# A one-core hybrid block with a gathered expert mixer: expert slots in pairs through TensorE's column halves, and a new order of slots, dots and front pieces

## The chip, the cores and the metric

The kernel runs on one core of a Trainium2 chip, in one launch. All tensors are float32. The metric is the device time of the whole kernel in microseconds, as the median of several runs. Before the change that is 3865.39 us (3 runs, 3864.82 to 3865.42).

## The reference, cut to what matters

A sequence of 1024 tokens of width 1024 goes through a block with three stages: a token mixer (gated delta net and sliding-window attention side by side), a mixer of single-neuron experts, and a gated embedding. The change is in the expert mixer, and in how the rest is interleaved with it:

```
def block(xb):                                   # 128 tokens
    qr = (xb @ w_query).reshape(128, 8, 2, 128)
    s1, s2 = scores of the two halves of qr against 128 keys each, per head
    v1, i1 = lax.top_k(s1, 16);  v2, i2 = lax.top_k(s2, 16)
    cand = (v1[..., :, None] + v2[..., None, :]).reshape(128, 8, 256)
    sc, ci = lax.top_k(cand, 16)
    eid = e1 * 128 + e2                          # 8 heads x 16 = 128 experts for each token
    gate = jax.nn.softmax(sc, axis=-1)
    hid = jnp.einsum('thkd,td->thk', expert_u[eid], xb)
    act = jax.nn.gelu(hid, approximate=False) * gate
    return jnp.einsum('thk,thkd->td', act, expert_v[eid])
h = h + peer_experts(rms_norm(h, g_ffn), ...)
```

So each token has 128 slots. A slot needs two rows of 4 KB from tables in HBM (`expert_u[eid]` and `expert_v[eid]`), a dot product of length 1024 with the first, and a weighted sum of the second.

## The kernel before, in words

The tokens are cut into 8 tiles of 128. A tile has a **front** (norms, delta net, attention, output projection, query projection, top 16 twice, gates; split into "pieces" per engine) and an **expert phase** (128 slots in 16 groups of G = 8). The expert phase of tile t-1 is interleaved by hand, in program order on each engine, with the front of tile t: the function `tile(t)` of PE (L1184) and of DVE (L1656) alternates one group with one piece. Tiles 2 to 7 of the front are a hardware loop on each engine; tiles 0 and 1 are written out. The last expert phase has no front beside it, but the gated embedding stage.

One group goes like this:

- **POOL** (`gather_group`, L563) copies the group's 8 ids (L567), then issues 8 gathers of `u` rows and 8 of `v` rows (L576). One gather is one slot of all 128 tokens: 128 rows of 4 KB, one per partition. Both rings have 8 buffers. Before every second gather POOL waits until that buffer of the group before is free (`u_used`, `v_used`).
- **DVE** (`experts`, L1642) waits for each `u` row block and makes one dot per slot (L1645), 8 in a row, then waits for the gelu and multiplies by the gate (L1648). Only then does it go on with its front piece.
- **ACT** (`experts`, L813) does the gelu and then builds 8 diagonal matrices of 128x128 (weights of one slot on the diagonal), each after PE has used that buffer's predecessor.
- **PE** (`experts`, L1167) waits for each `v` block and each diagonal, and adds diagonal times rows to the sum in PSUM `expert_sum`: for each slot two matmuls of 512 columns. It does the group before its piece g: PE runs group g-1, then piece g. (In the trace a float32 matmul is two records.)

At the end of a tile DVE copies the new normed rows and gates over (`publish`, L1633), which can be done only when the last dot of the old tile is through, and POOL takes the new ids (`take_ids`, L579). The sum leaves PSUM in `experts_out` (L1650), two copies at L1654.

Pieces of the front that the prediction names: piece0 (PE turns 12 blocks, DVE norms), piece1 and decays_of (gates and decays), piece2 (scaled keys and queries, turned), piece3 and level 1 to 5 (inverse of a triangular matrix: PE, ACT, PE, ACT, PE, DVE for each level), piece6 and piece7 (state), attention_norm, piece8 to piece10 (attention), piece11 and project_out, residual and piece12 (norm), query_pair 0 to 3, best_pair 0 to 3 (top 16), pick (ids), gates.

## Time and profile before

| | |
|---|---|
| median of 3 runs | 3865.39 us |
| the profiled execution's span | 4090.1 us |
| PE busy | 3315.7 us, 81% |
| DVE busy | 2191.8 us, 54% |
| ACT busy | 992.4 us, 24% |
| POOL busy | 2278.2 us, 56% |
| read from HBM, written | 1190.61 MB, 20.77 MB |

The profiled execution is longer than the timed runs (4090.1 against 3865.39 us), so a time worked out in it has to be scaled. PE is TensorE (its weight loads stand apart as PEld), DVE VectorE, ACT ScalarE, POOL GpSimd, SP SyncE. A name as L894 is a line of the kernel; L894 is the helper through which nearly all matmuls go and L897 the one for transposes, so PE's groups are told apart by the tiles they write and read. "Idle before" is time in which the engine stood still ahead of instructions of that group, with what released it.

### The profile page before, as it was taken

Reading aid. Unit: us, or ns where it says so; the run is one execution under the profiler, and the core shown is the slowest. Engines: PE = TensorE matmul, PEld = TensorE weight load, DVE = VectorE, ACT = ScalarE, POOL = GpSimd, SP = SyncE. Lnnn points to the kernel's source line nnn. Section 1 sums busy time; section 2 is a strip of 40 time slices with the busy share of each in tenths; the row PEclk is TensorE's granted clock in tenths of the full one; section 3 lists DMA queues with packets and bytes.
Section 4 is the critical chain, followed back from the end, with each engine's and each line's share of the span. In section 5 each row is a group of like instructions: output and inputs, shape, how many; then the busy total and the mean of one; then the engine's idle time right before and its main releaser. Section 6 shows DMA issues by size and latency. Waiting matters only on the chain.

```text
span 4090.1 us, 38210 instructions
## 1 busy us (share of the span) xinstructions
PE 3315.7 (81%) x11032; PEld 1816.9 (44%) x11032; DVE 2191.8 (54%) x4881; ACT 992.4 (24%) x2278; POOL 2278.2 (56%) x2189
## 2 busy tenths in 40 slices
PE   8997757897788787887879778877888687969999
PEld 4444535453444344443535344444545253534444
DVE  1124285567444854477456744486357644574543
ACT  2112213222222132212221222212221222213332
POOL 0000055667556775767566755676566656666764
PEclk9998778898889897898889888898899798989999
DMA  3321187899789998899889978899799979999996
GB/s 125 118 75 63 39 298 263 309 363 389 264 302 335 362 358 289 316 346 365 280 313 373 365 269 297 318 360 342 278 324 369 356 260 322 352 364 373 381 355 243
DMA packets 413927, 1214.00 MB, mean 297 GB/s; under 512 B 43680, under 2 KB 137888, under 8 KB 413600
## 3 DMA queue, kind: packets, MB, share of 16 engines
q0 software_dynamic: 294912, 1073.87, 71.6%
q1 hardware_dynamic: 118816, 137.66, 9.9%
q8 instruction: 103, 1.69, 0.2%
q14 instruction: 96, 0.79, 0.1%
HBM read 1190.61 MB, written 20.77 MB: 296 GB/s over the span
## 4 chain that ended last, share of the span: by engine, by line
PE 54%; DVE 14%; issue 13%; DMA 7%; POOL 5%; ACT 4%; another core or an unknown queue 2%; SPq 1%; POOLq 0%; DVEq 0%; ACTq 0%
PE expert_sum L894 28%; PE bank L894 23%; DVE u_rows L1645 5%; DMA u_rows<-in_peer_u_dram,group_ids 4%; DMA w_query<-in_peer_w_query_dram 3%; PE bank L897 3%; POOL u_rows L576 3%; POOL v_rows L576 2%; ACT weight_diagonals L610 1%; ACT L610 1%; ACT arena L610 1%; DVE arena L1420 1%; DVE arena L1552 1%; DVE arena L1537 1%
## 5 line engine op out<-in xcount | busy, mean ns | idle before, releaser
L894 PE MATMUL expert_sum<-v_rows,weight_diagonals 128*128 128x512 f32 x4096 | 1871.7, 617 | 153.0 <-ACT weight_diagonals L610 116.9
L576 POOL DMA_INDIRECT v_rows<-in_peer_v_dram,group_ids x1024 | 1191.1, 1163 | 827.7 <-PE expert_sum L894 541.8
L1645 DVE CUSTOM_DVE_ANT_0 u_rows<-u_rows,ffn_in 128x1024 f32<-128x1024 f32 x1024 | 1215.7, 1225 | 454.8 <-DMA u_rows<-in_peer_u_dram,group_ids 410.3
L894 PEld LDWEIGHTS expert_sum<-v_rows,weight_diagonals 128*128 128x128 f32 x4096 | 810.4, 200 | 1161.7 <-issue 1078.0
L576 POOL DMA_INDIRECT u_rows<-in_peer_u_dram,group_ids x1024 | 1052.3, 1028 | 416.8 <-issue 371.0
L897 PE MATMUL bank<-constants,arena 128*128 128x128 f32 x968 | 184.5, 336 | 330.2 <-DVE arena L1475 82.4
L610 ACT ACTIVATE weight_diagonals<-constants,expert_weight 128x128 f32<-128x128 f32 x1024 | 331.7, 390 | 228.5 <-PE expert_sum L894 177.4
L894 PE MATMUL bank<-w_query,arena 128*128 128x256 f32 (+1 forms) x1088 | 297.6, 436 | 87.4 <-DMA w_query<-in_peer_w_query_dram 50.6
L610 ACT ACTIVATE gelu<-hidden 128x8 f32<-128x8 f32 x128 | 26.7, 208 | 1386.1 <-DVE hidden L1645 1237.0
L897 PEld LDWEIGHTS bank<-constants,arena 128*128 128x128 f32 x968 | 139.1, 171 | 392.6 <-issue 212.2
L894 PEld LDWEIGHTS bank<-w_query,arena 128*128 128x128 f32 x1088 | 231.6, 215 | 155.7 <-issue 59.6
L589 POOL CAST expert_id<-expert_id_new 128x32 uint32<-128x32 f32 x1 | 0.2, 209 | 522.1 <-DVE expert_id_new L1602 522.1
L894 PE MATMUL bank<-arena 128*128 128x128 f32 (+4 forms) x2176 | 252.2, 295 | 40.1 <-issue 23.0
L894 PEld LDWEIGHTS bank<-arena 128*128 128x128 f32 (+3 forms) x2176 | 240.7, 201 | 60.5 <-issue 47.0
L894 PE MATMUL bank<-w_out_sb,arena 128*128 128x512 f32 x512 | 235.2, 615 | 21.9 <-ACT arena L861 10.4
L610 ACT ACT_TABLE_LOAD x172 | 220.7, 1283 | 3.8 <-PEq L1751 0.7
L1420 DVE COPY_PREDICATED arena<-constants,bank 128x512 f32<-128x512 uint32 x80 | 58.1, 726 | 287.3 <-PE bank L894 131.6
L894 PE MATMUL bank<-normed_by_channel,w_channel 128*128 128x512 f32 x384 | 167.2, 598 | 0.5 <-issue 0.5
L894 PEld LDWEIGHTS bank<-w_out_sb,arena 128*128 128x128 f32 x512 | 99.5, 197 | 146.7 <-issue 132.7
L894 PE MATMUL bank<-w_token,normed_tile 128*128 128x512 f32 (+1 forms) x384 | 142.4, 532 | 0.0
L1513 DVE TENSOR_TENSOR arena<-arena,bank 128x512 f32<-128x512 f32 x16 | 11.0, 688 | 203.5 <-PE bank L894 173.0
L894 PEld LDWEIGHTS bank<-normed_by_channel,w_channel 128*128 128x128 f32 x384 | 73.7, 193 | 93.6 <-issue 93.6
(166 smaller groups left out, 1968.1 us busy)
## 6 DMA issues: line engine op xcount, KB each, us to landing
w_query<-in_peer_w_query_dram SPq DMA_DIRECT2D x64, 1024.0 KB
u_rows<-in_peer_u_dram,group_ids POOLq DMA_INDIRECT x1024
v_rows<-in_peer_v_dram,group_ids POOLq DMA_INDIRECT x1024
w_channel<-in_w_in_dram SPq DMA_DIRECT2D x12, 512.0 KB
conv_scratch<-conv_out SPq DMA_DIRECT2D x12, 512.0 KB, 2.6
arena<-conv_scratch SPq DMA_DIRECT2D x8, 768.0 KB
tok_scratch<-token_out SPq DMA_DIRECT2D x8, 648.0 KB
arena<-tok_scratch SPq DMA_DIRECT2D x8, 648.0 KB
```

Source lines behind the costliest of these rows:

```text
L576: nc.gpsimd.indirect_dma_start(ring[:, j, :], None, table, bass.IndirectOffsetOnAxis(ids[:, half, j:j + 1], 0)).then_inc(landed[j], 16)
L589: nc.gpsimd.tensor_copy(eid[:, 0:EARLY * G], eid_new[:, 0:EARLY * G]).then_inc(first_ids_taken, 1)
L610: return nc.scalar.activation(out_, in_, func, **kw)
L894: return nc.tensor.matmul(out_, lhsT, rhs, start=start, stop=stop, **kw)
L897: return nc.tensor.transpose(out_, in_, ident)
L1420: v.copy_predicated(invT[:, 4 * r:4 * r + 4, :], level_mask(l), bank[3 + r][:, :].rearrange("p (s n) -> p s n", n=P)).then_inc(invT_ready, 1)
L1513: v.tensor_tensor(h1[:, n * 512:n * 512 + 512], x_t[:, n * 512:n * 512 + 512], bank[n][:, :], ALU.add).then_inc(h1_ready, 1)
L1537: last = v.max_index(index[:, first], top[:, first], row)
L1552: last = v.max_index(index[:, second], top[:, second], row)
L1645: v.tensor_tensor_reduce(u_ring[:, j, :], u_ring[:, j, :], xb[:], 1.0, 0.0, ALU.mult, ALU.add, hid[:, g * G + j:g * G + j + 1]).then_inc(u ...
```

## The change

1. **Paired slots.** The slots of one token are taken in pairs. PE turns ids, gates and normed rows over with identity halves (`ids_to_pairs`, `gates_to_pairs`, `rows_to_pairs`), so that partition 64 s + i of buffer j = 2m + b holds token 64 b + i and its slot 2m + s. A gather still fetches 128 rows. The weight matrix of a buffer is then 128x64 (two slots of 64 tokens), and its products go to the 64 partitions b of the sum. Four matmuls of 512 columns serve a pair of buffers, as before, but with 64 weight columns each, b = 0 and b = 1 in turn.
2. **Weights by DVE.** ACT no longer builds diagonals. DVE makes the weights of half a group with one multiplication of a constant 0/1 matrix (`C_REP`) with the weights, into two sets of buffers.
3. **Sums one group behind.** In step q, DVE begins with two dots of group q, then the weights of group q-1 (`begin`). PE does the slots of group q-1 in one block, then its piece. ACT's gelu of group q-1 comes in step q too.
4. **Dots spread.** The other six dots of a group are laid one or two at a time ahead of DVE's waits inside the front piece (`fill`); what is left follows the piece.
5. **Front re-cut** into pieces by new borders: piece9 with piece10, piece11 with project_out(1), level 5 with piece6 and piece7, and so on. The last step of a tile has no piece on any engine.
6. **POOL** issues in pairs, `v` of group q-1 and `u` of group q in turn, straight from `eid`, which has two sets now. The copies of ids and the `publish` copies are gone; ACT copies ids, gates and rows out of PSUM.
7. **No loops** over tiles are left in this part; everything is written out.
8. For the very first tile PE turns ids over only after all of its query pairs.

The core of the diff, PE and DVE:

```diff
-                for j in range(G):
-                    pe.wait_ge(v_landed[j], (t * NG + g + 1) * 16)
-                    pe.wait_ge(diag_ready, t * SLOTS + g * G + j + 1)
-                    for n in range(2):
-                        last = mm(acc[:, n * 512:n * 512 + 512], diag[:, j, :], v_ring[:, j, n * 512:n * 512 + 512],
-                                  False, g == NG - 1 and j == G - 1)
...
+                for pair in range(PAIRS):
+                    for b in range(NB):
+                        pe.wait_ge(v_landed[pair * NB + b], (q + 1) * 16)
+                    pe.wait_ge(diag_ready, 2 * q + (pair * NB) // GP + 1)
                     for n in range(2):
...
+                        for b in range(NB):
+                            last = mm(acc[b * B:b * B + B, n * 512:n * 512 + 512], diag[:, q % 2, pair * NB + b, :],
+                                      v_ring[:, pair * NB + b, n * 512:n * 512 + 512], False,
+                                      g == NG - 1 and pair == PAIRS - 1)
...
+            def expert_weights(q, half):
...
+                dve.wait_ge(gelu, 2 * q + half + 1)
+                v.tensor_tensor(act_w[:, q % 2, cols], gel[:, q % 2, cols], gate[:, e % 2, g * G + cols.start:g * G + cols.stop],
+                                ALU.mult).then_inc(weights_ready, 1)
+                dve.wait_ge(weights_ready, 2 * q + half + 1)
...
+                v.tensor_tensor(diag[:, q % 2, cols, :], cst[:, C_REP:C_REP + B].unsqueeze(1).broadcast_to([P, GP, B]),
+                                act_w[:, q % 2, cols].unsqueeze(2).broadcast_to([P, GP, B]), ALU.mult).then_inc(diag_ready, 1)
...
+            def begin(q):
+
+                fill(2)
+                if q:
+                    expert_weights(q - 1, 0)
+                    expert_weights(q - 1, 1)
...
             def level(t, l):
                 for r in range(2):
+                    fill(2 if r == 0 else 1)
                     dve.wait_ge(level_p, 10 * t + 2 * (l - 1) + r + 1)
...
+            for q in range((NT - 1) * NG):
+                dots = expert_dots(q)
+                begin(q)
...
+                for i in front_piece(q):
+                    pieces[i](q // NG + 1)
+                fill(G)
```

and POOL:

```diff
+            for q in range(NP):
+                e, g = divmod(q, NG)
+                late = e > 0 and g == 0
...
+                for pair in range(PAIRS):
+                    if q and not late:
+                        gather_v(q - 1, pair)
+                    gather_u(q, pair)
```

PE's main loop: for each q, the block of slots of group q-1 (`finish_slots`), then the piece. In steps 14 and 15 of a tile PE turns ids, gates and rows over. `fill` stands in PE's pieces too, but the block ahead of the piece has taken all slots by then.

## Rows read from the trace of the kernel before

**Rows 1.** Groups by line and shape: busy us, mean ns, idle before.

```profile
L894 PE MATMUL expert_sum<-v_rows,weight_diagonals 128*128 128x512 f32 x4096 | 1871.7, 617 | 153.0 <-ACT weight_diagonals L610 116.9 <-issue 36.0
...
L1564 DVE TENSOR_TENSOR arena<-arena 128x256 f32<-128x256 f32 x64 | 24.4, 424 | 14.2 <-remote 10.0 <-DVE arena L1552 3.4
...
L1648 DVE TENSOR_TENSOR expert_weight<-gelu,gate 128x8 f32<-128x8 f32 x128 | 21.9, 171 | 35.2 <-ACT gelu L610 32.2 <-issue 3.0
```

**Rows 2.** Timeline of DVE: the sum leaves PSUM, tiles 0 and 5.

```profile
1001.53 1.29 DVE L1654 COPY ffn_in_new<-expert_sum 128x512 f32<-128x512 f32 x2
...
3228.07 1.29 DVE L1654 COPY ffn_in_new<-expert_sum 128x512 f32<-128x512 f32 x2
```

**Rows 3.** Windows: us; busy PE, PEld, DVE, ACT, POOL; clock, DMA share, GB/s.

```profile
1450.00:1895.00 445.00, 357.48 (x1230) 201.03 (x1231) 260.96 (x594) 110.55 (x271) 292.20 (x277) 0.88 0.91 330
...
3671.00:4060.00 389.00, 360.44 (x871) 162.30 (x871) 189.60 (x320) 113.92 (x229) 257.33 (x258) 0.96 0.96 365
```

**Rows 4.** Timeline of PE in a steady tile: blocks of slots.

```profile
1511.32 13.90 PE L894 MATMUL expert_sum<-v_rows,weight_diagonals 128*128 128x512 f32 x32
...
1539.76 15.54 PE L894 MATMUL expert_sum<-v_rows,weight_diagonals 128*128 128x512 f32 x32
```

**Rows 5.** Who waited for whom: total us, times, longest us.

```profile
POOL v_rows L576 <- PE expert_sum L894: 541.8, 195, 22.7
...
DVE u_rows L1645 <- DMA u_rows<-in_peer_u_dram,group_ids: 410.3, 216, 13.3
```

**Rows 6.** Timeline of PE: a front product in column halves begins, twice.

```profile
468.35 0.45 PE L894 MATMUL bank<-arena,values_before 128*64 128x128 f32 x4 [0.68 <-ACT arena L768]
...
1675.53 0.70 PE L894 MATMUL bank<-arena,values_before 128*64 128x128 f32 x4 [0.68 <-ACT arena L768]
```

**Rows 7.** Windows over those two products, columns as in rows 3.

```profile
468.30:470.30 2.00, 1.95 (x32) 1.78 (x32) 0.00 (x0) 0.00 (x0) 0.00 (x0) 1.00 0.04 8
...
1675.50:1679.00 3.50, 3.47 (x32) 3.34 (x32) 0.00 (x0) 0.00 (x0) 2.21 (x4) 0.50 0.89 308
```

**Rows 8.** Timeline of DVE: dots; a best_pair; pick and gates.

```profile
573.04 1.23 DVE L1645 CUSTOM_DVE_ANT_0 u_rows<-u_rows,ffn_in 128x1024 f32<-128x1024 f32 x1
...
574.19 1.22 DVE L1645 CUSTOM_DVE_ANT_0 u_rows<-u_rows,ffn_in 128x1024 f32<-128x1024 f32 x1
...
505.40 0.87 DVE L1532 MAX8 arena<-arena 128x8 f32<-128x128 f32 x4 [15.36 <-ACT arena L797]
...
516.89 0.20 DVE L1576 CAST arena<-arena 128x64 f32<-128x64 uint32 x1
...
1410.47 0.23 DVE L1576 CAST arena<-arena 128x128 f32<-128x128 uint32 x1
...
1420.89 1.22 DVE L1645 CUSTOM_DVE_ANT_0 u_rows<-u_rows,ffn_in 128x1024 f32<-128x1024 f32 x1
```

**Rows 9.** Timelines of PE and DVE: front of tile 0, without experts.

```profile
367.02 2.80 PE L897 MATMUL bank<-constants,arena 128*128 128x128 f32 x12 [16.11 <-DMA arena<-conv_scratch]
...
401.14 0.73 DVE L1420 COPY_PREDICATED arena<-constants,bank 128x512 f32<-128x512 uint32 x1 [5.16 <-PE bank L894]
...
406.40 0.73 DVE L1420 COPY_PREDICATED arena<-constants,bank 128x512 f32<-128x512 uint32 x1 [3.59 <-PE bank L894]
...
503.52 1.33 PE L894 MATMUL bank<-keys_by_channel,arena 128*128 128x128 f32 x8
```

**Rows 10.** Timeline of PE: two levels with experts beside, written out.

```profile
681.68 3.78 PE L894 MATMUL bank<-arena 128*128 128x128 f32 x32
...
693.75 13.90 PE L894 MATMUL expert_sum<-v_rows,weight_diagonals 128*128 128x512 f32 x32
```

**Rows 11.** Timelines of POOL and PE: first gather; end of tile 0's queries.

```profile
523.98 1.09 POOL L576 DMA_INDIRECT u_rows<-in_peer_u_dram,group_ids  x1 [0.94 <-POOL group_ids L567]
...
535.78 0.94 PE L894 MATMUL bank<-keys_by_channel,arena 128*128 128x128 f32 x4 [0.71 <-issue]
```

**Rows 12.** Windows: the 25 us with the densest DMA, columns as in rows 3.

```profile
1800.00:1825.00 25.00, 17.05 (x54) 11.10 (x52) 20.62 (x59) 3.96 (x14) 17.67 (x17) 0.86 1.03 401
```

More of the change, by code:

```diff
@@ L607, in _ @@
+            for pair in range(PAIRS):
+                gather_v(NP - 1, pair)
         @block.scalar
@@ L827, in _, with experts @@
+            def experts(q):
+                for half in range(2):
+                    cols = slice(half * GP, half * GP + GP)
+                    act.wait_ge(u_used, q * G + cols.stop)
+                    f(gel[:, q % 2, cols], hid[:, q % 2, cols], ACT.Gelu).then_inc(gelu, 1)
+            first, rest, whole = slice(0, EARLY * G), slice(EARLY * G, SLOTS), slice(0, SLOTS)
+            for piece in pieces[:9]:
                 piece(0)
             normed_T(0)
-            for pair in range(3):
+            for pair in range(4):
@@ L830, in _ @@
                 query_pair(0, pair)
-            piece_gate(0, slice(0, EARLY * G))
-            query_pair(0, 3)
-            for g in range(FIRST):
-                experts(0, g)
-            piece_gate(0, slice(EARLY * G, SLOTS))
-            for i, group in enumerate(merged(pieces)):
-                experts(0, FIRST + i)
-                for piece in group:
-                    piece(1)
-            with act.Fori(2, NT) as t:
-                for g in range(NG):
-                    experts(t - 1, g)
-                    pieces[g](t)
+            take_rows(0)
@@ L1191, in _, with fill, finish_slots @@
+            slots = iter(())
+            credit = 0
+            def fill(n):
+                nonlocal credit
+                credit += n
+                while credit >= 2:
+                    credit -= 2
+                    next(slots, None)
+            def finish_slots():
+                for _ in slots:
+                    pass
             pe.wait_ge(rel_rows_ready, NH)
+            first, rest, whole = slice(0, EARLY * G), slice(EARLY * G, SLOTS), slice(0, SLOTS)
             for piece in pieces:
@@ L1193, in _ @@
                 piece(0)
-            for g in range(FIRST - 1):
-                experts(0, g)
-            for i, group in enumerate(merged(pieces)):
-                experts(0, FIRST - 1 + i)
-                for piece in group:
-                    piece(1)
-            experts(0, NG - 1)
-            with pe.Fori(2, NT) as t:
-                tile(t)
+            rows_to_pairs(0)
+            ids_to_pairs(1, first)
+            pe.wait_ge(first_gates, 1)
+            gates_to_pairs(first)
@@ new lines, in _ @@
+            for q in range((NT - 1) * NG):
+                t = q // NG + 1
+                slots = expert_slots(q - 1) if q else iter(())
+                credit = 0
+                if q % NG == NG - 1:
+                    rows_to_pairs(t)
+                finish_slots()
+                for i in front_piece(q):
+                    pieces[i](t)
+                if q == 1:
+                    ids_to_pairs(3, rest)
+                    pe.wait_ge(vector_front, 1)
+                    gates_to_pairs(rest)
+                if q % NG == NG - 2:
+                    ids_to_pairs(2 * t + 3, whole)
+                    pe.wait_ge(vector_front, t + 1)
+                    gates_to_pairs(whole)
@@ L1650, in experts_out, with fill @@
+            dots = iter(())
+            def fill(n):
+                for _ in range(n):
+                    next(dots, None)
+            def begin(q):
+                fill(2)
+                if q:
+                    expert_weights(q - 1, 0)
+                    expert_weights(q - 1, 1)
+                if q > NG and q % NG == 1:
+                    experts_out(q // NG - 1)
             def experts_out(t):
[L1652 removed]
+                dve.wait_ge(v_used, (t + 1) * SLOTS // NB)
+                if t < NT - 1:
+                    dve.wait_ge(rows_mm, 2 * NB * (t + 2))
```

388 lines of the change are left out of this document (225 added, 163 removed).

## The prediction

> **What bounds the kernel now.** I read the page's costly groups first, then the stretches by tile, the order of blocks and pieces on PE, and the waits. PE is busy for 1871.7 us of the 4090.1 with the products of the experts' sum, 128 groups of 14.6 us [rows 1]. A steady tile takes 445.3 us: the sum leaves PSUM at 1001.53 and, five tiles on, at 3228.07 [rows 2]. In such a tile PE is busy 357 of 445 us and the DMA engines 0.91 at 330 GB/s; in the last one, without a front, PE has 360 of 389 us and DMA 0.96 at 365 GB/s [rows 3]. PE runs a block of slots (13.9 to 15.5 us), then its piece: from the block's end at 1525.2 the next begins at 1539.76, 14.5 us for two levels [rows 4]. The largest waits behind PE are POOL's for free `v` buffers (541.8 us); DVE's for `u` rows are 410.3 us [rows 5]. So PE's chain of block and piece sets the steady time, with DMA close behind, and DVE sets the stretch with the top 16.
>
> **Part 1, the block of slots.** The number of matmuls stays at 2048, but two with 64 columns of weights can run side by side. A front product has this form already, 128 rows by 64 weight columns, 128 moving columns, halves in turn: beginning at 468.35 and at 1675.53 [rows 6]. Its 32 records keep PE busy for 1.95 us at a granted clock of 1.00 and for 3.47 us at 0.50 [rows 7], so at full clock a record comes every 0.061 us, while a record of a full array costs 13.90 / 32 = 0.434 us for 512 columns [rows 4], 0.109 for 128. That is a factor of nearly 2. No row shows it with 512 moving columns. Bounds for a block: 14.6 us (no gain) and 7.0 (half of 13.9); I take 7.3, half the mean, since the row nearest in form has the full factor. The work is off PE for 117 us a tile.
>
> **Part 2, what is late next.** Before, the weights of group g-1 were there when PE came, and DVE's end of a piece ran beside PE's block. Now PE's block in step q waits for `begin(q)` on DVE, which comes after DVE's whole piece of step q-1: two dots at 1.15 (573.04 to 574.19), a product of 0.17, a weight build of 256 columns, for which I take the 0.42 of a sum of that size, and an estimated 0.3 for the waits between: 3.2 us [rows 1, 8]. Then the block, then PE's piece, then DVE's end of it, in series. So a step costs the piece's bare chain plus 3.2 plus 7.3. The bare chain is to be seen in tile 0, whose front ran with no experts: from the first turn at 367.02 to the scores of query pair 0 at 504.85 it took 137.8 us [rows 9]. That is steps 0 to 9:
> - bare chain 137.8; less 5 for products of piece2 and for attention_norm, which DVE can do beside PE's block;
> - ten blocks: 73;
> - ten times 3.2 ahead of the block, less 3.7 in step 8, where PE is still turning probabilities: 28;
> - dots laid in waits that don't hide them. DVE idles 3.59 us ahead of a level, which holds two dots of 1.15; the third one, between the two halves of a level, costs 1.1, five times; some ten others stand in gaps about as short as themselves, an estimated 1 each: together 15 [rows 8, 9];
> - h1 added to the sum, four records of 0.43: 2;
> - delays that the bare chain doesn't have: two levels took 12.1 us from 681.68 to 693.75 with experts beside them, in written-out code [rows 10], against 10.5 alone (401.14, two levels at 5.26) [rows 9]. I take 15% of 137.8: 20.
>
> Sum 271 us. Bounds of the last term: 0, and 38% (14.5 against 10.5) as in the loop [rows 4], 52.
>
> **Part 3, steps 10 to 14 belong to DVE.** 40 dots 46; five times the weights of both halves 7.5; four best_pair at 11.5 (505.40 to 516.89) 46; two picks and the gates, 10.4 (1410.47 to 1420.89) and 9: 19.4; split dots 2; less 4, as step 10 begins beside PE's step 9: 117 [rows 1, 8]. Nothing is gained there, and ACT's builds of diagonals go from an engine with room. **Step 15** has no piece: DVE and PE are soon done and the round of 16 gathers decides. A gather is 0.524 MB; at 365 / 0.96 = 380 GB/s [rows 3] it takes 1.38 us, 22 for the round. Some short steps (2, 9) reach this floor too: 4.
>
> A steady tile then takes 271 + 117 + 22 + 4 = 414 us, 31.3 less, six times: -188. POOL's copies of ids and the drain at the end of a tile are in this difference. The unrolled code and two more sets of buffers cost nothing that a row shows; two levels took less in written-out code than in the loop, 12.1 against 14.5 [rows 4, 10].
>
> **Part 4, the ends.** The first gather now goes out at 523.98, while PE's queries of tile 0 last until 536.7 [rows 11]. After the change ids are turned over only after these, the turned rows (8 matmuls, 3.5 us in halves) and some copies by ACT: near 545, 21 to 22 us later, and DVE stands still for it: +22. Expert phase 0, mostly without the loop already: 0, bounds -30 and +30. The last tile now takes 24.3 us a step with PE at 93% [rows 3]; with a block of 7.3 the DMA round of 22 us is the next limit: 16 x 22.1 + 2 = 356 against 389: -33. The sum one group behind at the very end: +3.
>
> Sum: 4090.1 - 188 + 22 + 0 - 33 + 3 = 3894 us profiled. The median is 0.9451 of the profiled span (3865.39 / 4090.1); scaled, 3680 us.
>
> **Rivals.**
> - *DMA is the bound.* If DVE's ends of pieces hide better than in my sum, transfers limit: a tile moves 445 x 330 = 146.9 MB [rows 3], at 380 GB/s 386 us; the densest 25 us moved 401 GB/s [rows 12], which gives 366. With 386: 4090.1 - 356 + 22 - 30 - 33 + 3 = 3696, scaled 3493 (with 366: 3380). For it: DMA already has a share of 0.91. Against: the series in part 2.
> - *The new wait takes back all of it.* If the pieces stretch by 38% as in the loop, the tile is 446 us: 4090.1 + 4 + 22 + 20 - 33 + 3 = 4106, scaled 3881. For it: dots wait for `u` rows ahead of the front's work on DVE, so that a late gather now holds the front as well (410.3 us of such waits) [rows 5].
> - *Slower: PE's clock.* PE will stand still more, ahead of each block above all. In the stretch at 1675.5, after PE had waited for probabilities, the granted clock was 0.50 [rows 7], its lower level of 1.2 GHz, and records took twice as long. A block at half clock lasts 14 us. With two thirds of the ten blocks' time so, 44 us are added: tile 458, 4090.1 + 76 + 22 + 30 - 33 + 3 = 4188, scaled 3958. It decides from a mean block of 10.4 us on (31.3 / 10 more than 7.3). Against: blocks now lose 0.7 us on average (14.6 against 13.9) though PE waits ahead of them too [rows 1, 4].
> - *The halves don't run side by side at 512 columns.* Ten blocks cost 73 us more: tile 487, last tile as before: 4090.1 + 250 + 22 + 50 + 3 = 4415, scaled 4173.
>
> The Trainium skill, TensorE: Matmul & The Clock Gate, Part 1, says that the array's clock is gated by activity and that gaps between bursts bring it back to the half rate; by that rule, which the row at 1675.5 bears out, the clock rival holds and 3958 us is its time. The Trainium skill, DMA: Bandwidth & Descriptors, Specifications, gives a limit of about 358 GB/s from HBM per core, by which a tile could not go below 410 us and the DMA rival would be out; the last tile's mean of 365 GB/s disagrees [rows 3], and the measurement decides.
>
> **How the numbers follow.** The forecast (tile of 400 to 432 us) gets 0.53; the DMA bound 0.15; the new wait 0.17; the clock 0.10; no concurrency 0.05. The range, 3470 to 3890 us, reaches from just under the DMA case to just over the new wait's; it leaves out the two slow cases and the far end of the fast one, some 0.2. The bounds of the 15% term alone are 3567 and 3862 (six tiles of -20 and +32 us, scaled). A measurement of this kernel tells 0.2% from no change. Faster: forecast and DMA case, and 0.07 of the new wait: 0.75. Within 0.2%: 0.05. Slower: 0.20.
>
> **What would show it.** In the profile of the changed kernel: blocks of 32 records in 7 to 8 us (over 10: clock; 14: no concurrency); PE's products of the sum near 940 us; between piece and block on PE a wait of 3 us for DVE's weights; steps 5, 7 and 8 the longest, over 28 us; the sum leaving PSUM every 414 us; DMA near 355 GB/s in a steady tile; the first gather near 545. A tile under 395 us with a DMA share near 1 would make part 2 wrong; a DVE that waits for `u` rows inside its pieces would make the second rival right.

## The result, and the profile after

The changed kernel took 4007.3 us (median; 3987.2 to 4008.0) beside 3865.4 for the kernel before: a ratio of 1.035, 95% interval 1.033 to 1.037. It is slower by 142 us. The forecast was 3680 us, so the change came out 327 us above it.

From its page and its groups (answering to [rows 1]): the span; the busy share of each engine; the shares of the chain of work that ended last; then the group of the sum with out<-in, shape and count, busy us and mean ns of one, idle time before them and what ended it.

```profile
span 4005.3 us, 34568 instructions
...
PE 2609.5 (65%) x11304; PEld 1355.7 (34%) x11304; DVE 2239.5 (56%) x5248; ACT 688.0 (17%) x1425; POOL 2323.0 (58%) x2052
...
PE 42%; DVE 22%; DMA 18%; issue 11%; POOL 4%; ACT 3%; SPq 1%; DVEq 0%; POOLq 0%; ACTq 0%
...
L920 PE MATMUL expert_sum<-v_rows,weight_diagonals 128*64 128x512 f32 x4096 | 1135.0, 710 | 837.2 <-DVE weight_diagonals L1765 678.0
```

The halves do run side by side: PE's busy time in the sum fell from 1871.7 us to 1135.0, a mean block from 14.6 to 8.87 us (1135.0 / 128). But PE now waits 678 us for DVE's weights, and its busy share of the span fell from 81% to 65%. Who waited for whom, in all (total us, times, longest), beside [rows 5]:

```profile
PE expert_sum L920 <- DVE weight_diagonals L1765: 678.0, 121, 29.7
...
POOL v_rows L591 <- PE expert_sum L920: 386.6, 86, 30.7
...
DVE u_rows L1780 <- DMA u_rows<-in_peer_u_dram,expert_id: 310.0, 124, 13.1
...
PE expert_sum L920 <- DVE ffn_in_new L1807: 93.1, 7, 13.9
```

Windows over a steady tile and the last one, columns as in [rows 3], and DVE's timeline where the sum leaves PSUM after the first tile, the seventh and the last:

```profile
1465.90:1892.40 426.50, 263.23 (x1253) 138.30 (x1253) 264.64 (x637) 68.58 (x153) 293.51 (x256) 0.79 0.93 341
3607.00:3977.00 370.00, 287.52 (x868) 113.24 (x868) 187.76 (x346) 71.96 (x110) 256.92 (x240) 0.88 0.96 364
```

```profile
1039.74 1.28 DVE L1807 COPY ffn_in_new<-expert_sum 128x512 f32<-128x512 f32 x2
...
3607.21 1.28 DVE L1807 COPY ffn_in_new<-expert_sum 128x512 f32<-128x512 f32 x2
...
3977.44 1.29 DVE L1807 COPY ffn_in_new<-expert_sum 128x512 f32<-128x512 f32 x2 [11.77 <-PE expert_sum L920]
```

Six steady tiles are 3607.21 - 1039.74 = 2567.5 us, 427.9 each, and the last one is 370.2.

One thing must be known to read these numbers: the same program takes different times on different chips. The execution of the kernel before that stands ahead of the prediction lasts 4090.1 us, its timed runs 3865.4; those of the change agree with its profile (4005.3 and 4007). The experiments met two kinds of chip: on A (the result's), D and F the kernel before takes 3865 to 3874 us, on B, C and E 4084 to 4132. The profile of before that the prediction read is like those of the second kind. What differs is shown under experiments 2 and 3; numbers are compared here on one chip, or on chips where the kernel before takes the same. Each letter stands for one chip at one time: no run tells whether the chip itself makes the difference or something that happened there then, such as other work beside it.

### The profile page after: what moved, and what is told of

Read it like the earlier page. It is cut to its first block, busy times and chain, and to the rows that moved or that the text cites. A ratio compares the mean times of both kernels' runs of the same rounds, so it can differ in the third digit from the quotient of the medians.

```text
span 4005.3 us, 34568 instructions
## 1 busy us (share of the span) xinstructions
PE 2609.5 (65%) x11304; PEld 1355.7 (34%) x11304; DVE 2239.5 (56%) x5248; ACT 688.0 (17%) x1425; POOL 2323.0 (58%) x2052
## 4 chain that ended last, share of the span: by engine, by line
PE 42%; DVE 22%; DMA 18%; issue 11%; POOL 4%; ACT 3%; SPq 1%; DVEq 0%; POOLq 0%; ACTq 0%
PE bank L920 23%; PE expert_sum L920 16%; DMA w_query<-in_peer_w_query_dram 11%; DVE u_rows L1780 7%; DMA v_rows<-in_peer_v_dram,expert_id 3%; DMA u_rows<-in_peer_u_dram,expert_id 3%; POOL u_rows L582 2%; PE bank L923 2%; POOL v_rows L591 2%; DVE arena L1530 1%; ACT L616 1%; DVE arena L1713 1%; DVE arena L1719 1%; DVE arena L1722 1%; ACT arena L616 1%
## 5 line engine op out<-in xcount | busy, mean ns | idle before, releaser
L582 POOL DMA_INDIRECT u_rows<-in_peer_u_dram,expert_id x1024 | 1196.3, 1168 | 967.4 <-ACT expert_id L821 539.4
L920 PE MATMUL expert_sum<-v_rows,weight_diagonals 128*64 128x512 f32 x4096 | 1135.0, 710 | 837.2 <-DVE weight_diagonals L1765 678.0
L591 POOL DMA_INDIRECT v_rows<-in_peer_v_dram,expert_id x1024 | 1126.5, 1100 | 675.8 <-PE expert_sum L920 386.6
L1780 DVE CUSTOM_DVE_ANT_0 u_rows<-u_rows,ffn_in 128x1024 f32<-128x1024 f32 x1024 | 1222.5, 1218 | 313.1 <-DMA u_rows<-in_peer_u_dram,expert_id 310.0
L920 PEld LDWEIGHTS expert_sum<-v_rows,weight_diagonals 128*64 128x64 f32 x4096 | 367.7, 161 | 1551.8 <-issue 1551.4
L923 PE MATMUL bank<-constants,arena 128*128 128x128 f32 x968 | 171.3, 318 | 251.7 <-DVE arena L1625 85.9
L920 PE MATMUL bank<-arena 128*128 128x128 f32 (+4 forms) x2176 | 234.9, 282 | 18.6 <-DVE arena L1530 13.4
L920 PEld LDWEIGHTS bank<-arena 128*128 128x128 f32 (+3 forms) x2176 | 222.7, 189 | 42.6 <-issue 26.2
L1759 DVE TENSOR_TENSOR expert_weight<-gelu,gate 128x4 f32<-128x4 f32 x256 | 40.6, 159 | 280.7 <-ACT gelu L616 280.6
L795 ACT COPY arena<-bank 128x256 f32<-128x256 f32 x64 | 23.8, 372 | 583.6 <-PE bank L920 583.6
L1765 DVE TENSOR_TENSOR weight_diagonals<-constants,expert_weight 128x256 f32<-128x256 f32 x256 | 108.9, 426 | 8.8
```

The lines of the kernel that those rows point to most:

```text
L582: nc.gpsimd.indirect_dma_start(u_ring[:, j, :], None, table_u, bass.IndirectOffsetOnAxis(id_of(q, j), 0)).then_inc(u_landed[j], 16)
L591: nc.gpsimd.indirect_dma_start(v_ring[:, j, :], None, table_v, bass.IndirectOffsetOnAxis(id_of(q, j), 0)).then_inc(v_landed[j], 16)
L920: return nc.tensor.matmul(out_, lhsT, rhs, start=start, stop=stop, **kw)
L923: return nc.tensor.transpose(out_, in_, ident)
L1759: v.tensor_tensor(act_w[:, q % 2, cols], gel[:, q % 2, cols], gate[:, e % 2, g * G + cols.start:g * G + cols.stop], ALU.mult).then_inc(wei ...
L1765: v.tensor_tensor(diag[:, q % 2, cols, :], cst[:, C_REP:C_REP + B].unsqueeze(1).broadcast_to([P, GP, B]), act_w[:, q % 2, cols].unsqueeze( ...
```

## The experiments

All runs under one heading were made on one chip, with the kernel before beside them.

### 1. Chip B (before: 4131 us): loops, and three ways to undo the wait

The kernel before with its loops over tiles written out:

```diff
-            with pe.Fori(2, NT) as t:
+            for t in range(2, NT):
```

> The kernel before with the loops over tiles 2 to 7 (and POOL's over groups) written out on all five engines, nothing else changed. The profiled execution of before lasts 4090.1 us, its timed runs 3865.4; the change, whose tiles are written out, lasts 4005.3 profiled and 4007 timed. Theory L (loops cost time only while they are profiled): the timed run stays near 3865 (within 10 us), the profiled span falls to within 10 us of it, a steady tile then shows about 408 us (445.3 less 225 / 6) and two levels take about 12 us where the loop's took 14.5. Rival M (loops help the unprofiled run, for instance by shorter code to fetch): the timed run rises to about 4000. Rival N (the difference comes from POOL's copies of ids or ACT's diagonals, which the change drops, not from loops): the profiled span stays near 4090 with a timed run near 3865.

Measured: 4093.7 us, ratio 0.991 (0.988 to 0.994), profiled span 4080.1. None of the three theories holds. The profiled span and the time of this kernel agree, and the kernel before takes 4131 here. Loops cost some 37 us on this chip; they are not where the 225 us between profile and time lie.

Dots and weights of a group in its own step, as before the change:

```diff
 def begin(q):
-    fill(2)
-    if q:
-        expert_weights(q - 1, 0)
-        expert_weights(q - 1, 1)
+    fill(G)
+    expert_weights(q, 0)
+    expert_weights(q, 1)
```

> The change, but DVE does all 8 dots of group q, then its weights and diagonals, at the head of step q, ahead of its piece (as before the change), and ACT its GELU there; PE still sums group q-1 in step q, in column halves. PE then finds the weights ready. Theory W (the series DVE piece, two dots, weights, PE block, PE piece is what the change lost; it waits 678 us for weights): these waits fall under 150 us, the steady tile of 426 us goes to about 400, the time to about 3830. Rival S (the dots spread over the piece's waits are worth as much as the wait costs): the steady tile stays within 8 us of 426, the time between 3950 and 4060. Rival D (DMA, at a share of 0.93, is the bound): tile no lower than 415, time no lower than 3920.

Measured: 4333.9 us, ratio 1.049 (1.038 to 1.060). PE's wait for weights fell to 7 us in all, and the time is that of the change (4338 on chip C, where before takes the same 4132). That is what rival S foretold, that eight dots ahead of DVE's piece put into the series what the wait took out. But this run changes a second thing. DVE copies the sum out only behind its eight dots and weights, and PE waits for that copy before it can begin the next tile's sum; first this run, then the change on C:

```profile
PE expert_sum L918 <- DVE ffn_in_new L1804: 255.9, 7, 40.5
...
PE expert_sum L920 <- DVE ffn_in_new L1807: 94.0, 7, 14.4
```

So 162 us of new waits stand at the seven tile borders, and how much of the rest the dots took is not separated.

PE sums two groups behind (POOL fetches the `v` rows one step later too, and DVE copies the sum out one step later):

```diff
-                slots = expert_slots(q - 1) if q else iter(())
+                slots = expert_slots(q - 2) if q > 1 else iter(())
```

> The change, but PE sums the slots of group q-2 in step q (and POOL gathers their v rows there), so that the weights made in step q-1 are there when PE comes; dots stay spread. Theory W: the 678 us of waits for weights mostly go, about half of them, 340 us, leave the path: steady tile about 395, time about 3800. Rival D (DMA bound): tile 410 to 420, time 3890 to 3960, DMA share 0.96 or more. Rival C (what follows is DVE's and PE's chain of the piece anyway, so only PE's place of waiting moves, to its first turn or product of each piece): time 3980 to 4010, waits for arena tiles on PE grow by what those for weights lose.

Measured: 4121.4 us, ratio 0.997 (0.994 to 1.001). Against the change's 1.051 on chip C that is 5% won back without moving a dot. The times of 3800 (theory W) and 3980 to 4010 (rival C) were meant for a chip of the first kind; experiment 5 has that run.

PE's slots in the waits of its piece:

```diff
-                finish_slots()
                 for i in front_piece(q):
                     pieces[i](t)
+                finish_slots()
```

> The change, but PE's slots of a group are laid in the waits of its piece (a pair of slots at every second place marked there, what is left at the piece's end) and not as one block ahead of it. Theory W: PE's piece still stands behind weights, but only a pair of slots of 2.2 us lies between it and DVE's next operation, so the block leaves the chain in steps with several turns: steady tile 426 less about 20, time about 3870. Rival B (a block is the better place: v buffers come free later, and pairs of slots hold up turns for which DVE waits): time 4030 or more, POOL's waits for v buffers above 387 us.

Measured: 4006.9 us, ratio 0.969 (0.961 to 0.976), 8% under the change's ratio on C. Theory W in kind: of the single choices undone on this chip, the block ahead of the piece cost the most.

### 2. Chip C (before: 4132): the two kernels again, and the change taken apart

> The kernel before, unchanged, for its own trace beside a time of the same chip. On one chip its timed runs took 3865 us (within 1 us of each other), on the chip of the written-out version, another one, 4107 to 4179, and the profiled span of 4090 us is like the latter. Theory K (the kernel before has two speeds, by chip, and the trace that the forecast was read from is of the slower one): the profiled span equals the time of its own chip within 30 us, whichever that is; where it is near 3865, the trace shows which stretch is shorter. Rival P (a profile costs 225 us on the fast chip): span near 4090 beside times near 3865.

> The change, unchanged, on the same chip as the kernel before. It took 4007 us where before took 3865. Theory K: before is the one that varies, the change stays within 30 us of 4007, so that on a chip where before takes 4130 the change is faster by 3%, and on one where before takes 3865 slower by 3.5%. Rival: the change varies as before does, the ratio stays 1.035, and the time on the slower chip is near 4275.

Measured: before 4130.9 us, profiled span 4117.8; the change 4337.8, ratio 1.051 (1.045 to 1.056). Theory K held for the profile and fell for the change: it varies as before does, and more (8% against 7%). Its two executions, on A and C, are the same program. Up to the first gather they agree within 0.4 us (539.9 and 540.2); after it a tile takes 428 us on A and 471 on C. The engines' own durations are alike: a dot has a mean of 1218 and 1219 ns, a record of the sum 710 and 714. The timeline of all engines shows what differs. First chip A: PE's products of a level, ACT's two copies, then DVE's masked copy, which waits for PE's second product:

```profile
1550.68 3.88 PE L920 MATMUL bank<-arena 128*128 128x128 f32 x32
...
1551.87 0.58 ACT L731 COPY arena<-bank 128x512 f32<-128x512 f32 x1 [11.32 <-PE bank L920]
...
1552.77 0.59 ACT L731 COPY arena<-bank 128x512 f32<-128x512 f32 x1 [0.31 <-PE bank L920]
...
1553.82 0.73 DVE L1530 COPY_PREDICATED arena<-constants,bank 128x512 f32<-128x512 uint32 x1 [9.18 <-PE bank L920]
```

And the same place on chip C, with a window over it:

```profile
1613.63 3.15 PE L920 MATMUL bank<-arena 128*128 128x128 f32 x24
...
1614.98 0.59 ACT L731 COPY arena<-bank 128x512 f32<-128x512 f32 x1 [12.51 <-PE bank L920]
...
1619.29 0.59 ACT L731 COPY arena<-bank 128x512 f32<-128x512 f32 x1 [3.72 <-remote]
1619.93 0.97 PEld L920 LDWEIGHTS bank<-arena 128*128 128x128 f32 x8 [3.34 <-issue]
...
1625.12 0.72 DVE L1530 COPY_PREDICATED arena<-constants,bank 128x512 f32<-128x512 uint32 x1 [17.24 <-remote]
```

```profile
1615.50:1625.50 10.00, 2.44 (x18) 1.94 (x16) 0.38 (x1) 0.66 (x2) 5.49 (x6) 0.81 1.02 401
```

PE had ended the 24 products at 1616.8 us; ACT's copy, due 0.3 us after its half, started 3.7 us late, and DVE's, due at 1617, at 1625.1, though both engines stood idle. The semaphore's own record has its change at 1625.0: the signal landed late. "Remote" and "issue" in such rows name no engine; they mean that no end of work stands beside the change.

How often this happens can be counted. For each of the 5268 signals that PE, DVE and ACT raise after the first gather I took the next recorded change of its semaphore: in the trace of C it comes over 0.5 us after the instruction's end for 1167 of them, on A for 3. (An upper bound, as records are missing: C's trace lists 31,042 changes of semaphores, A's 42,917 for the same program.) The trace of before that the prediction read is of the late kind too, with 1637 of 6229 by the same count. So are all twelve traces taken on B, C and E, with 16 to 34%; the six of A, D and F have three such signals at most.

The change without column halves:

```diff
-B = 64
+B = 128
```

> The change without its column halves: one slot at a time with 128 columns of weights, as in the kernel before; everything else of the change stays (dots spread, sums one group behind, slots as one block ahead of the piece, weights on DVE). A block lasts 13.9 to 15 us. Theory B (in the series of steps 0 to 9 the block's length counts in full): 128 blocks x 5.5 us less what hides in steps 10 to 15, some 10 of 16 steps in 7 tiles, the last tile too: 4007 + 7 x 55 + 60 = 4450 us. Rival H (half of a block hides beside DVE's work): 4200. Against the kernel before this shows what spreading and the later sum cost or bring by themselves: faster than before only if under its time.

Measured: 4794.7 us, 457 over the change on this chip. A mean block has 2041.6 / 128 = 15.95 us instead of 8.9:

```profile
L920 PE MATMUL expert_sum<-v_rows,weight_diagonals 128*128 128x512 f32 x4096 | 2041.6, 662 | 707.8 <-DVE weight_diagonals L1765 482.3 <-issue 206.7 <-DMA v_rows<-in_peer_v_dram,expert_id 18.8
```

Theory B: ten blocks in each of seven tiles are 70 x 7.0 = 491 us. In the order of the change the block stands in the series nearly in full. And without the halves that order is 663 us slower than before on this chip; the halves only pay for part of it.

Weights ahead of the dots:

```diff
 def begin(q):
-    fill(2)
     if q:
```

> The change, but the weights of group q-1 come first in DVE's step q, not behind two dots of group q. Theory W (two dots of 1.2 us are in the series ahead of the block): in ten steps of a tile 2.4 us less, of which about 1.2 come back as waits for ACT's GELU: 12 us a tile, 80 to 90 in all, time 3920. Rival R (DVE then waits for the GELU as long as the dots last, or the dots taken out have to be done later in the same series): no change within 15 us of the change's own time.

Measured: 4338.0 us, the change's own time. Rival R: the two dots cost nothing where they are. Without them DVE waits longer for ACT's GELU, 444 us in all by the rows of waits (246 ended by ACT, 197 by nothing named) against 301 in the change on C.

### 3. Chip D (before: 3870): the kernel before, traced on a chip without late signals

> The kernel before, unchanged, again for the trace of a further chip. So far two chips gave 4131 us and one 3865. In the traces of the slow ones a part of the engines' signals land late: a semaphore that PE raised at 1616.8 us reached DVE at 1625.0, where the trace of the change at 4007 us shows delays of 0.01 us throughout. Theory K2 (late signals make the slow chips slow, for every kernel): where the time is near 3865, the trace shows no share of issue and unknown queue above that of the change's fast trace (11%), two levels in the loop take about 10.5 to 12 us instead of 14.5, and a steady tile takes about 408 to 415 us; where it is near 4130, the trace is as the two before it (445 to 450 a tile).

Measured: 3874.2 us, span 3861.4. Theory K2. Of 6228 signals one is late by the count above. Windows over a steady tile and the last, and PE's timeline over two levels:

```profile
1397.40:1811.20 413.80, 346.61 (x1225) 193.32 (x1224) 260.38 (x591) 105.99 (x260) 289.26 (x275) 0.90 0.95 350
3462.70:3832.00 369.30, 355.88 (x869) 160.62 (x870) 183.32 (x308) 113.40 (x228) 248.10 (x250) 0.98 0.97 370
```

```profile
1459.71 13.90 PE L894 MATMUL expert_sum<-v_rows,weight_diagonals 128*128 128x512 f32 x32
1473.45 3.78 PE L894 MATMUL bank<-arena 128*128 128x128 f32 x32
...
1483.91 13.90 PE L894 MATMUL expert_sum<-v_rows,weight_diagonals 128*128 128x512 f32 x32
```

A tile has 413 us (986.4 to 3462.7 in six), not 445. Two levels in the loop take 24.20 - 13.90 = 10.3 us, not the 14.5 of [rows 4], and in the written-out tile 1 they take 10.5 (671.86 to 682.32), not the 12.1 of [rows 10]; tile 0 alone has 10.5. What the prediction took for the loop's price and for the company of experts were late signals.

> The change with PE's slots laid in the waits of the piece, as in the earlier run (4007 us where the kernel before took 4131, ratio 0.969). Theory W (the block ahead of the piece is what the change lost, on any chip): ratio 0.95 to 0.98 on a slow chip again; on a fast one, where the change takes 4007 and before 3865, 3800 to 3860. Rival B (the gain comes only from cover against late signals): on a fast chip not faster than the change's 4007.

> The change with both: PE sums group q-2 in step q, and its slots lie in the waits of the piece (h1 is added at the head of the step). Theory W: neither weights nor the block stand in the series any more, only pairs of slots of 2.2 us that hold up a turn by one on average: 20 to 60 us under the version with slots in the pieces alone, near 3960 on a slow chip, 3760 on a fast one. Rival D (that version is bound by DMA already, whose share of its steady tile is to be 0.93 or more): no change against it within 15 us.

Measured: 3874.8 us, ratio 1.000 (0.998 to 1.002), and 3840.9 us, ratio 0.991 (0.988 to 0.994). On this kind of chip slots in the pieces bring 132 us against the change's 4007 on A and merely reach the kernel before, above theory W's 3800 to 3860; rival B is out. With the sums two groups behind as well the kernel before is beaten, by 0.9%: 34 us under the slots alone, as theory W had it, though far from its 3760. Windows of that last version, a steady tile and the last one (15 steps, as the sum leaves a step later):

```profile
1442.70:1846.10 403.40, 276.19 (x1253) 138.07 (x1253) 266.95 (x636) 68.73 (x153) 291.92 (x254) 0.81 0.96 359
3473.00:3814.00 341.00, 270.26 (x843) 102.41 (x843) 176.00 (x325) 66.58 (x103) 253.03 (x227) 0.90 0.98 376
```

### 4. Chip E (before: 4084): what a halved block is worth by itself

In the kernel before, each slot goes into half of the sum's columns, so that the block is halved and the other half of the columns lacks its experts:

```diff
-                    for n in range(2):
+                    for n in range(2 if g == NG - 1 and j == G - 1 else 1):
                         last = mm(acc[:, n * 512:n * 512 + 512], diag[:, j, :], v_ring[...],
```

> The kernel before (loops, order, full-array slots unchanged) with half of its slots' work left out: each slot is multiplied into columns 0 to 511 of the sum alone (the last slot of a tile into both halves), so that a block lasts 7 us instead of 13.9, as column halves at full clock would make it; the other half of the sum's columns lacks its experts. It measures what a halved block is worth with nothing else of the change. Theory B (the block is in PE's series in ten steps of a tile): 48 to 69 us less a tile, near 3480 where the kernel before takes 3870, near 3740 where it takes 4131. Theory D (on the fast chip a tile of 412 us has the DMA engines at 0.95 already, and 16 rounds of gathers at 23 us leave 370 to 400): tile about 400, time 3760 to 3800 there, and a larger gain, 100 to 250 us, on a slow chip, where DMA has more room.

> The change with PE's sums two groups behind and its slots in the waits of the piece, again: 3841 us on a fast chip (0.991 of before). Theory T (this order has slack for signals that land late, as the version with slots in the pieces alone, which lost 132 us on the slow chip where before lost 261): on a slow chip 3950 to 4000 and a ratio of 0.955 to 0.97; on a fast one 3830 to 3850 again. Rival: it loses as much as before, 4100.

> The change with PE's sums two groups behind, the slots still as one block: 4121 us on a slow chip, where the change takes 4337. Theory W (waits for weights cost the change 5% on any chip): on a fast chip 3850 to 3900 against the change's 4007. Rival L (two thirds of those 216 us are late signals that fall on the added wait): 3930 to 3970 on a fast chip. On a slow one 4110 to 4130 again.

> The change, unchanged, beside the three others of this call on one chip: 4007 us where the kernel before takes 3870, 4337 where it takes 4131.

Measured: half block 4027.3 us, ratio 0.987 (0.981 to 0.994); both measures 3913.5, 0.959 (0.953 to 0.965); two behind alone 4099.6, 1.004 (1.001 to 1.008); the change 4350.3, 1.062 (1.054 to 1.070). The half block gave 57 us, less than either theory: with late signals two levels took 30.1 and 25.8 us. The order that wins on D wins by more here: it is 73 us slower than on D, where the kernel before is 214 slower and the change, against A, 343. Its trace has no fewer late signals than that of the change (32% against 20%). That they cost most where waits stand in one series fits these numbers; no run singles it out.

### 5. Chip F (before: 3867): the same two without late signals

> As the run before it with half of the slots' work left out (each slot into columns 0 to 511 alone), which gave 4027 us where the kernel before took 4084: there pieces grew by as much as blocks shrank, two levels took 26 to 30 us with signals that landed late. On a chip without late signals: theory D (DMA at 0.95 to 0.97 of the kernel before bounds it) gives 3790 to 3830 where before takes 3870; theory B (PE's series) under 3600. On a chip with late signals near 4030 again.

> As the run of the change with PE's sums two groups behind and one block, which gave 4100 where the change took 4350. On a chip without late signals theory W gives 3850 to 3900 (the change 4007), rival L 3930 to 3970; on a chip with them 4100 again.

Measured: half block 3735.1 us, ratio 0.965 (0.963 to 0.967); two behind 3884.8, 1.005 (1.003 to 1.008), in theory W's range and 122 us under the change on A. Most of the 678 us of waits did not become time: PE still stands 596 us ahead of the sum's products (837 in the change), 526 of them ended by nothing that the profile names. By the code PE waits there for `v` rows and for weights, and the weights were made a step earlier. Here 24 records run and the 8 of the last pair of `v` buffers come after 3.6 us:

```profile
1522.29 5.37 PE L921 MATMUL expert_sum<-v_rows,weight_diagonals 128*64 128x512 f32 x24
...
1531.29 3.10 PE L921 MATMUL expert_sum<-v_rows,weight_diagonals 128*64 128x512 f32 x8 [3.63 <-issue]
```

So 122 us is what a later sum with later `v` gathers brings; the price of the wait for weights by itself was not measured.

PE's timeline over two levels of the half-block kernel, ACT's in the same step, and windows over a steady tile, that step and the last tile:

```profile
1433.02 7.03 PE L894 MATMUL expert_sum<-v_rows,weight_diagonals 128*128 128x512 f32 x16
1439.88 1.95 PE L894 MATMUL bank<-arena 128*128 128x128 f32 x16
1446.12 3.78 PE L894 MATMUL bank<-arena 128*128 128x128 f32 x16 [4.28 <-ACT arena L725]
...
1456.74 7.03 PE L894 MATMUL expert_sum<-v_rows,weight_diagonals 128*128 128x512 f32 x16
```

```profile
1442.63 0.21 ACT L610 ACTIVATE gelu<-hidden 128x8 f32<-128x8 f32 x1 [8.83 <-DVE hidden L1645]
1443.15 2.44 ACT L610 ACTIVATE weight_diagonals<-constants,expert_weight 128x128 f32<-128x128 f32 x8 [0.31 <-DVE expert_weight L1648]
1445.50 1.04 ACT L725 COPY arena<-bank 128x512 f32<-128x512 f32 x2
```

```profile
1391.00:1788.00 397.00, 254.55 (x967) 153.54 (x967) 261.10 (x590) 104.21 (x260) 290.54 (x274) 0.79 0.98 367
...
1433.00:1456.70 23.70, 19.06 (x98) 14.10 (x97) 12.88 (x22) 7.11 (x17) 17.46 (x20) 0.86 1.03 408
3364.70:3718.60 353.90, 271.21 (x615) 123.33 (x616) 182.85 (x308) 113.47 (x228) 246.84 (x251) 0.85 1.00 388
```

The block is 6.9 us shorter and the step 0.5 us: 23.72 against 24.20. Two things took the rest. In the order before, DVE does its eight dots while PE does its block, and ACT then does the GELU and builds eight diagonals (2.44 us) ahead of its copy for the level; with half the block gone PE stands 4.3 us for that copy. And of the level's products the 16 behind this wait take 3.78 us where the 16 ahead of it took 1.95: the granted clock is 0.86 in the step, 1.00 in the same step on D. The change has no diagonals on ACT, so this run prices a halved block in the kernel before and not in the change.

A steady tile has 398 us in the mean of six (394 to 405), 14 us less than on D, with the DMA engines at 0.98. Theory D was right about the tile (about 400) and 55 us too high in its time (3790 at the least); B is out. That transfers bound this tile is read from their share; no run varied them.

## Why the prediction was wrong

**The scale to the runs.** This is the step that failed, and it made two thirds of the miss: 3894 - 3680 = 214 us. The factor 0.9451 was 3865.39 / 4090.1, and it was laid on a sum whose largest terms had nothing to be scaled: the start of tile 0 (first gather at 524.0 in the trace that was read, 523.0 on D), blocks (13.90 in both) and dots are the same on both kinds of chip. The gap was in the late signals of the trace, and those lie in the tile of 445 us that the forecast tile replaced. On a chip without them the kernel before has 413 us, and the forecast of 414 was no gain at all. So it does not hold that a time worked out in that trace has to be scaled. Left unscaled, the prediction's own sum says 3894 beside 3865: slower. The warning was in the table of times: timed runs within 1 us of each other and a profiled execution 225 us away can't be one condition.

**The sum by terms**, forecast against the change's trace, with the kernel before on D. The forecast column lays the prediction's differences (-188, +22, -33, +3) on the rows of the trace that it read, where the sum leaves at 1001.5, 3682.9 and 4059.4:

| stretch, us | forecast | change (A) | before (D) |
|---|---|---|---|
| until the first tile's sum leaves | 1023.5 | 1039.7 | 986.4 |
| six steady tiles | 2493.4 | 2567.5 | 2476.3 |
| last tile | 343.5 | 370.2 | 369.3 |
| after it | 33.7 | 27.9 | 29.4 |
| span | 3894.1 | 4005.3 | 3861.4 |

The third of the miss that is left, 4005 against 3894 unscaled, is in the first three lines and is taken part by part.

**Part 1** held in kind. No row had shown halves with 512 columns side by side; they run so, and at full clock a block takes 7.09 us (the one at 1765.80), as taken. The mean is 8.87, since a block begins after a wait. The records of the sum (ns min/median/max), and a window over a step of two levels:

```profile
L920 PE MATMUL expert_sum<-v_rows,weight_diagonals x4096: 592/593/1117, 573.6 to 3976.3; 128*64 128x512 f32 x196
```

```profile
1541.90:1565.30 23.40, 18.88 (x112) 12.25 (x113) 12.80 (x25) 4.88 (x10) 18.52 (x17) 0.93 0.98 361
```

Half the records take 593 ns or less, the longest 1117, and the mean is 710 (607 in the kernel before on D). In a step of two levels the granted clock is 0.93, with DVE's wait in it, where it was 1.00 in the same step before. The rule of the Trainium skill, TensorE: Matmul & The Clock Gate, Part 1, holds in direction: gaps between bursts cost clock. The clock rival, which it carried, decided from 10.4 us on; at 8.87 it took 10 x 1.57 = 16 us a tile, and is a part of the loss, not its cause. The front's products paid nothing: those with `w_query` have a mean of 427 ns in both.

**Part 2, steps 0 to 9**, was nearly right as an absolute sum: 271 us forecast, 263.5 measured (blocks at 1442.67 and 1706.20). Its terms in a step of two levels, PE's timeline of the change:

```profile
1541.96 8.78 PE L920 MATMUL expert_sum<-v_rows,weight_diagonals 128*64 128x512 f32 x32 [2.23 <-DVE weight_diagonals L1765]
1550.68 3.88 PE L920 MATMUL bank<-arena 128*128 128x128 f32 x32
1554.60 0.66 PE L923 MATMUL bank<-constants,arena 128*128 128x128 f32 x4
1556.35 0.66 PE L923 MATMUL bank<-constants,arena 128*128 128x128 f32 x4 [1.10 <-DVE arena L1530]
...
1565.30 8.78 PE L920 MATMUL expert_sum<-v_rows,weight_diagonals 128*64 128x512 f32 x32 [2.23 <-DVE weight_diagonals L1765]
```

The step has 23.34 us where before has 24.20: the block is 5.1 us less; from the last product to the block there are 2.88 us, 2.4 more than before, for the weights; and 0.86 more in each of the two levels, where a dot lies between the halves of DVE's masked copy (1554.60 to 1556.35, 1.75 us; before 0.89). The excess of 15% isn't there: two levels take 10.3 us plus those 4.1. It made up for the longer blocks. What the prediction missed is what the step was to be compared with: before, the block lay beside DVE's dots, and the step was PE's and DVE's at once. The half-block run shows it for the kernel before, where half a block gives this step 0.5 us.

The term for h1 was mis-sized: it had four records, 2 us, where PE waits in each tile as well, 93.1 us in seven:

```profile
1893.74 3.78 PE L920 MATMUL expert_sum<-arena,constants 128*128 128x512 f32 x4 [13.88 <-DVE ffn_in_new L1807]
```

The sum can't restart before DVE has copied it out, and DVE comes to that only after the last six dots of step 0, two of step 1 and the weights (1881.6 to 1892.4). This wait is part of the 263.5.

**Part 3** missed by 13 us in steps 10 to 14 (129.9 against 117) and by 7 in step 15 (32.9, from 1836.1 to the block at 1869.0, against 22 and 4). Windows over both:

```profile
1706.20:1836.10 129.90, 77.28 (x324) 40.30 (x325) 107.80 (x329) 11.23 (x33) 90.30 (x78) 0.82 0.99 368
1836.10:1870.00 33.90, 11.57 (x36) 3.45 (x38) 11.87 (x22) 2.34 (x6) 22.37 (x23) 0.70 1.03 403
```

DVE is busy for 107.8 of 129.9 us, and the DMA engines are full. With one set of buffers they cannot fetch ahead in steps 0 to 9 (their share is 0.90 from 1466 to 1706) and, so it seems, become the limit in the rest; no run with more buffers tells.

In the last tile the prediction read its baseline wrongly: its window of 389 us begins 12 us before the sum leaves, and by the sum the tile is 376.5. So its 16 rounds of 22.1 and 2 (356) became 343.5 in the sum. Measured are 370.2, that is 23.1 us a round at 364 GB/s, as before on D. The round of 22.1 itself is reached: the half-block kernel's last tile takes 353.9 us at a share of 1.00 and 388 GB/s. So the 380 GB/s, from busy share and rate, holds for a tile without a front. Beside a front no steady tile shown here moves more than 367.

**Part 4.** The start: first gather at 539.9, forecast near 545, 17 us later than the 523.0 of D. Expert phase 0 was put at nothing and costs 1039.7 - 986.4 - 17 = 36 us; no run tells which of its steps lose it.

**The rivals.** "The new wait takes back all of it" is what happened, and its price, 3881 us after scaling, was 126 short. PE waits 678 us for weights, and the runs two groups behind give 122 us back on a chip without late signals and 216 to 251 with them. That it put the tile at 446 was the late signals again; it is 428. DMA as the bound fits what could be won, with another number: steady tiles have 398 us in the half-block kernel at a share of 0.98 and 406 in the best whole one, where 386 was priced. That halves don't run side by side fell. On every chip where it ran, the change is slower (1.035, 1.051, 1.062).

The Trainium skill, DMA: Bandwidth & Descriptors, Specifications, has about 358 GB/s per core; here the mean is 367 over a steady tile of 397 us and 388 over a last tile of 353.9, so the measurement differs and decides. As a bound for a tile (410 us by it) it was passed too, with the 398 and 406 above; the 386 was not reached.

## What to carry to other kernels

Before a profiled execution is scaled to the timed runs, ask what the gap is made of; a sum built from bare durations has no such gap, and must be compared with a baseline taken in the same condition. Halving an engine's block is worth what the block has in the series: where other engines work beside it, first read what they do in the same time (here half a block gave a step 0.5 of 6.9 us). And an order that puts weights, block and piece in one series can cost more than the halved block brings: on chip C the order cost 663 us and the halves won back 457. With the sum one group later still and the block cut into the waits of the piece, 3.5% slower (A) became 0.9% faster (D), and 6.2% slower became 4.1% faster (E).

## What the runs showed of the hardware that was not expected

- One program's time differs from chip to chip: the kernel before takes 3865 to 3874 and 4084 to 4132 us (5.4 to 6.9%), the change 4007 and 4338 to 4350 (8.2 to 8.6%), the order with both measures 3841 and 3913 (1.9%). The engines' own durations are alike. The difference is signals between engines that land late once gathers run, 8.2 us late in the case followed above. One such stretch had the DMA engines at 1.02 and 401 GB/s; but chip A has 403 GB/s at 1.03 without a late signal, so density alone is not the cause. What delays them stays open, and so does whether it belongs to the chip or to the time; no run varied either.
- Written-out loops were worth 37 us of 4131, 0.9% (0.6 to 1.2), on a chip with late signals.
- Products of 64 weight columns with 512 moving columns run in pairs side by side: 7.09 us for 32 records where 32 of a full array take 13.90.
